# Gated networks of a two-block transformer step: the high weights multiply the high and the low input in one 512-column product

## What is computed

```
def _swiglu(xn, w_gate, w_up, w_down):
    return (jax.nn.silu(xn @ w_gate) * (xn @ w_up)) @ w_down
```

## Time and profile before

| | |
|---|---|
| median of 3 runs | 1210.81 us (1208.66 to 1210.96) |
| span of the profiled execution | 1209.8 us |
| TensorE busy | 1182.0 us, 98% of the span |
| VectorE (DVE), ScalarE (ACT) busy | 744.9 us (62%), 596.8 us (49%) |
| mean granted TensorE clock | 0.995 of full speed |
| `ffn1`: first product after the transposes to the first of `down1` | 608.84 to 718.35 us |
| `ffn2`: first product after the transposes | 1005.28 us |

### The profile page before, as it was taken

The page is one execution under the profiler, slowest core; times in us unless marked ns, Lnnn a source line. Parts: engine busy times, 40 slices in busy tenths (PEclk is TensorE's granted clock), DMA queues, the critical chain, the costliest instruction groups (busy, mean ns, idle before and its releaser), DMA issues.

```text
span 1209.8 us, 20515 instructions
## 1 busy us (share of the span) xinstructions
PE 1182.0 (98%) x8276; PEld 1101.8 (91%) x8276; DVE 744.9 (62%) x893; ACT 596.8 (49%) x804; POOL 118.1 (10%) x165
## 2 busy tenths in 40 slices
PE   7999999999998999999999999999999999999997
PEld 7998899999877999988999998789999989999875
DVE  5867556565856697864555454565766476554455
ACT  5675453445545576553454443454464355443342
POOL 5310201001025000000000000100400010000011
PEclk9999999999999999999999999999999999999999
DMA  8644343446545576555375555465465548655541
GB/s 234 208 142 137 105 140 122 123 140 222 182 136 174 155 221 195 178 199 183 122 244 178 189 189 177 152 207 179 140 213 196 166 140 263 195 177 174 196 139 64
DMA packets 156019, 208.57 MB, mean 172 GB/s; under 512 B 8608, under 2 KB 127405, under 8 KB 155949
## 3 DMA queue, kind: packets, MB, share of 16 engines
q1 hardware_dynamic: 152781, 198.92, 51.9%
q10 hardware_dynamic: 3072, 8.65, 2.1%
q0 software_dynamic: 96, 0.01, 0.1%
HBM read 206.50 MB, written 1.05 MB: 172 GB/s over the span
## 4 chain that ended last, share of the span: by engine, by line
PE 91%; DVE 4%; ACT 2%; POOL 1%; issue 1%; DMA 1%; POOLq 0%; DVEq 0%; SPq 0%; ACTq 0%
PE ACCP L776 26%; PE ACCP L778 26%; PE ACCP L777 26%; PE SMP L927 3%; PE SMP L920 2%; PE SMP L776 2%; PE SMP L778 2%; PE SMP L777 2%; DVE LO L1893 1%; ACT HI L1395 1%; POOL STAT L652 1%; DMA PRE_GAIN<-in_norm_mix_dram 1%; POOL STAT L651 0%; DVE XS L1929 0%; DVE X L2362 0%
## 5 line engine op out<-in xcount | busy, mean ns | idle before, releaser
L1893 DVE TENSOR_TENSOR LO<-RAW,HI 128x1024 fp32r<-128x1024 f32 x361 | 432.8, 1238 | 244.1 <-ACT HI L1395 242.8
L1395 ACT ACTIVATE HI<-RAW 128x1024 fp32r<-128x1024 f32 x366 | 368.4, 1053 | 225.5 <-PE ACCP L778 206.5
L776 PE MATMUL ACCP<-XH,HI 128*128 128x256 f32 x1536 | 437.4, 285 | 2.0 <-DVE XL L1938 2.0
L778 PE MATMUL ACCP<-XH,LO 128*128 128x256 f32 x1536 | 435.3, 283 | 0.0
L777 PE MATMUL ACCP<-XL,HI 128*128 128x256 f32 x1536 | 435.3, 283 | 0.0
L776 PEld LDWEIGHTS ACCP<-XH,HI 128*128 128x128 f32 x1536 | 295.4, 192 | 2.3 <-DVE LO L1893 2.2
L777 PEld LDWEIGHTS ACCP<-XL,HI 128*128 128x128 f32 x1536 | 295.5, 192 | 0.0
L778 PEld LDWEIGHTS ACCP<-XH,LO 128*128 128x128 f32 x1536 | 295.4, 192 | 0.0
L776 PE MATMUL ACCP<-HI,HH 128*128 128x512 f32 x264 | 105.0, 398 | 0.0
L778 PE MATMUL ACCP<-HI,HL 128*128 128x512 f32 x264 | 104.7, 396 | 0.0
L777 PE MATMUL ACCP<-LO,HH 128*128 128x512 f32 x264 | 104.6, 396 | 0.0
(11 more groups left out here) (388 smaller groups left out, 1560.3 us busy)
## 6 DMA issues: line engine op xcount, KB each, us to landing
RAW<-in_w_in_dram SPq DMA_DIRECT2D x104, 512.0 KB, 4.5
RAW<-in_w_up_dram SPq DMA_DIRECT2D x44, 512.0 KB, 4.5
RAW<-in_ffn_w_gate_dram SPq DMA_DIRECT2D x44, 512.0 KB, 4.7
RAW<-in_ffn_w_up_dram SPq DMA_DIRECT2D x44, 512.0 KB, 4.6
RAW<-in_ffn_w_down_dram SPq DMA_DIRECT2D x44, 512.0 KB, 4.2
RAW<-in_w_down_dram SPq DMA_DIRECT2D x22, 512.0 KB, 3.9
RAW<-in_w_out_dram SPq DMA_DIRECT2D x8, 512.0 KB, 4.5
RAW<-in_w_mkv_dram SPq DMA_DIRECT2D x8, 512.0 KB, 5.1
```

The lines of the kernel that those rows point to most:

```text
L776: pe.matmul(dst, lhs[0], rhs[0], start=start, stop=False)
L778: return pe.matmul(dst, lhs[1], rhs[0], start=False, stop=stop)
L1395: act.activation(HI[:, n % RING, half_of(half)], RAW[:, n % RAWS, half, :], ACT.Copy).then_inc(hi_ready, 1)
L1893: dve.tensor_tensor(LO[:, s, c], RAW[:, n % RAWS, half, :], HI[:, s, c].bitcast(f32), ALU.subtract).then_inc(lo_ready[s], 1)
```

## The change

For the blocks of `ffn1` and `ffn2` behind the opening (19 and 18 of them), the high and the low input become one tensor `XHL`, and the high weights multiply both in one product with 512 columns; the low weights multiply the high input as before. So each half of a block takes a whole PSUM bank, with the part of the low input in its second 256 columns, and a block takes two banks: an even block banks 0 and 1, an odd one banks 2 and 3. ACT copies the second parts of both banks to a new buffer `CROSS`, DVE adds them to the first parts (two additions of 128x256, which free the banks), and Silu and the gating product then work in SBUF. The opening's transposes also put each block's halves into two banks, and Silu and product of those blocks become two instructions of 128x256 each. Block one's `up` phase and all others stay as they are.

```diff
+CROSSED = ("ffn1", "ffn2")
+        elif phase in CROSSED:
+            for j in range(count):
+                acc(phase, j, j, 2 * (j % 2), 2 * (j % 2) + 1)
...
-        XH = sb("XH", [P, KT, SEQ], f32r)
-        XL = sb("XL", [P, KT, SEQ], f32r)
+        XHL = sb("XHL", [P, 2, KT, SEQ], f32r)
+        XH, XL = XHL[:, 0], XHL[:, 1]
...
+            def f_crossed(phase, t):
+
+                s = lo_is_ready(pe, phase, t)
+                acc_banks_free(pe, phase, t)
+                for half in range(2):
+                    bank = acc(phase, t, half)
+                    whole = bank.rearrange("p (n s) -> p n s", s=SEQ)
+                    for k in range(KT):
+                        c = slice(k * 256 + half * P, k * 256 + half * P + P)
+                        if k < KT - 1:
+                            pe.matmul(whole, HI[:, s, c], XHL[:, :, k, :], start=k == 0, stop=False)
+                            pe.matmul(bank[:, 0:SEQ], LO[:, s, c], XH[:, k, :], start=False, stop=False)
+                        else:
+                            pe.matmul(bank[:, 0:SEQ], LO[:, s, c], XH[:, k, :], start=False, stop=False)
+                            last = pe.matmul(whole, HI[:, s, c], XHL[:, :, k, :], start=False, stop=True)
+                last.then_inc(block_done, 1)
...
                     for half in range(2):
                         for t in range(NT):
-                            dst = acc(phase, Turn(j))[:, half * SEQ + t * P:half * SEQ + (t + 1) * P]
+                            if phase in CROSSED:
+                                dst = acc(phase, Turn(j), half)[:, t * P:(t + 1) * P]
+                            else:
+                                dst = acc(phase, Turn(j))[:, half * SEQ + t * P:half * SEQ + (t + 1) * P]
...
             def glu_steps(phase):
+                def cross(t, k):
+
+                    acc_is_done(act, phase, t.part(k, 2))
+                    act.activation(CROSS[:, k], acc_pair(phase, t.part(k, 2), 1), ACT.Copy).then_inc(cross_ready, 1)
+
                 def step(t):
-                    a, b = t.part(0, 2), t.part(1, 2)
-                    acc_is_done(act, phase, a)
-                    act.activation(UA[:, t.j % 2], acc(phase, a).rearrange("p (n s) -> p n s", s=SEQ),
-                                   ACT.Silu).then_inc(acc_bank(phase, a), 1)
-                    split_behind(phase, a)
+                    a, b, u = t.part(0, 2), t.part(1, 2), t.j % 2
+                    if is_open(phase, a):
+                        acc_is_done(act, phase, a)
+                        for i in range(2):
+                            act.activation(UA[:, u, i, :], acc(phase, a, i)[:, 0:SEQ], ACT.Silu).then_inc(acc_bank(phase, a, i), 1)
+                        split_behind(phase, a)
+                    else:
+                        cross(t, 0)
+                        split_behind(phase, a)
+                        acc_is_taken(act, phase, a, 1)
+                        act.activation(UA[:, u], UA[:, u], ACT.Silu).then_inc(a_gated, 1)
+                    if not is_open(phase, b):
+                        cross(t, 1)
                     split_behind(phase, b)
-                    acc_is_taken(act, phase, b)
+                    act.wait_ge(h_ready, hidden_pairs(phase, t))
                     ffn_hi(t)
...
             def glu_steps(phase, pairs):
+                def whole(t, k, dst):
+
+                    part = t.part(k, 2)
+                    dve.wait_ge(cross_ready, crossings(phase, t, k))
+                    for i in range(2):
+                        dve.tensor_tensor(dst[:, i, :], acc(phase, part, i)[:, 0:SEQ], CROSS[:, k, i, :],
+                                          ALU.add).then_inc(acc_bank(phase, part, i), 1)
+
                 def step(t):
-                    a, b = t.part(0, 2), t.part(1, 2)
+                    a, b, u = t.part(0, 2), t.part(1, 2), t.j % 2
+                    if not is_open(phase, a):
+                        whole(t, 0, UA[:, u])
                     split_behind(phase, a)
-                    acc_is_done(dve, phase, b)
-                    acc_is_taken(dve, phase, a)
-                    dve.tensor_tensor(UB[:, t.j % 2], acc(phase, b).rearrange("p (n s) -> p n s", s=SEQ), UA[:, t.j % 2],
-                                      ALU.mult).then_inc(acc_bank(phase, b), 1)
+                    if is_open(phase, b):
+                        acc_is_done(dve, phase, b)
+                        for i in range(2):
+                            acc_is_taken(dve, phase, a, i)
+                            ins = dve.tensor_tensor(UB[:, u, i, :], acc(phase, b, i)[:, 0:SEQ], UA[:, u, i, :], ALU.mult)
+                            ins.then_inc(acc_bank(phase, b, i), 1)
+                        acc_is_taken(dve, phase, b, 1)
+                        dve.sem_inc(h_ready, 1)
+                    else:
+                        whole(t, 1, UB[:, u])
+                        if is_open(phase, a):
+                            acc_is_taken(dve, phase, a, 1)
+                        else:
+                            dve.wait_ge(a_gated, gatings(phase, t))
+                        acc_is_taken(dve, phase, b, 1)
+                        dve.tensor_tensor(UB[:, u], UB[:, u], UA[:, u], ALU.mult).then_inc(h_ready, 1)
                     split_behind(phase, b)
```

More of the change, by code:

```diff
@@ L304, in build @@
         UB = at("UB", 48, [P, 2, 2, SEQ])
+        CROSS = at("CROSS", 68, [P, 2, 2, SEQ])
         OPENED = at("OPENED", 56, [P, NT, 4 * 256])
@@ L375, in build @@
         post_sq, tap_done, dve_mix = sems("post_sq tap_done dve_mix")
+        cross_ready, a_gated = sems("cross_ready a_gated")
         ln_mean, ln_sq, ln_ready = sems("ln_mean ln_sq ln_ready")
@@ L448, in acc_is_done, with is_open, crossings, gatings @@
             eng.wait_ge(block_done, t.count(lambda j: ACC_LAST[phase, j] + 1))
+        def is_open(phase, t):
+            return t.i is None and t.j < F_OPEN[phase]
+        def crossings(phase, t, k):
+            before = sum(COUNT[p] - F_OPEN[p] for p in CROSSED[:CROSSED.index(phase)])
+            return t.count(lambda j: before + 2 * j + k + 1 - F_OPEN[phase])
+        def gatings(phase, t):
+            opened_a = [-(-F_OPEN[p] // 2) for p in CROSSED]
+            n = CROSSED.index(phase)
+            before = sum(FT // 2 - opened_a[i] for i in range(n))
+            return t.count(lambda j: before + j + 1 - opened_a[n])
+        def hidden_pairs(phase, t):
+            return t.count(lambda j: PAIRS.index(phase) * (FT // 2) + j + 1)
+        def acc_pair(phase, t, part):
+            b = ACC_BANKS[phase, t.j][0]
+            return ACCP[:, b:b + 2, part * SEQ:(part + 1) * SEQ]
         def tile_is_done(eng, phase, m):
@@ L1253, in ffn, with one @@
             def ffn(r, up, down, behind, before):
+                def one(t):
+                    if up in CROSSED:
+                        f_crossed(up, t)
+                    else:
+                        f_gemm(up, t, XH, XL)
                 def step(t):
                     for k in range(2):
-                        f_gemm(up, t.part(k, 2), XH, XL)
+                        one(t.part(k, 2))
                 def hidden_ready(k):
@@ L1262, in ffn @@
                 for j in range(F_OPEN[up], 4):
-                    f_gemm(up, Turn(j), XH, XL)
+                    one(Turn(j))
                 repeat(pe, 2, FT // 2, 2, step)
```

## The result

The changed kernel takes 1215.4 us (median), the kernel before 1211.2 us in the same series: a ratio of 1.0034, 95% interval 1.0023 to 1.0045. It is 4 us slower, where 2 us faster was forecast, and it lies above the forecast's range.

A forecast was written before the change was run, and what follows sets the result against it. The prediction took TensorE to bound the kernel. Wide products at -8.0 us, ACT and DVE at nothing and openings at +6.0 gave -2.0, from a 1210.8 us median to 1208.8 us, range 1207.0 to 1213.3.

The forecast's parts named there:

- What bounds the kernel: Whole kernel: 91% of the span lies on TensorE, so the distance between products and any added TensorE idle time count.
- Part 1, the wide product: Steady blocks of `ffn1` and `ffn2`: one 512-column product replaces two of 256, saving 13.5 ns in each of 592 steps, 8.0 us.
- 226.7 + 120.1: Steady blocks: one wide plus one narrow product makes a step of 346.8 ns, where three narrow ones took 360.3.
- home of the stationary side: Wide products: weights in tensors of their own (`HI`, `LO`) should cost 226.7 ns, those in the arena 234.1.
- The rule that the Trainium skill gives: Isolated products at full clock: columns over 2.4 plus about 2.5 ns; by it 592 steps would save only 1.5 us.
- Part 2, ACT and DVE in the steady blocks at nothing: Steady blocks: added copies and additions cost nothing, with cover of 3.7 us on the banks and 2.6 us on loads.
- Part 3, the openings: Starts of `ffn1` and `ffn2`: waits for banks to be freed by gating cost 2.5 + 3.5 = 6.0 us.
- The rival with the clock: Openings of `ffn1` and `ffn2`: TensorE's clock falls, 1.7 us lost; one fall gives 1210.5 us, two 1212.2; chance 0.20.
- The sum: Whole kernel: -8.0 + 6.0 = -2.0 us, so a forecast of 1208.8 us.
- The 234 ns rival: Steady blocks: the wide product costs 234.1 ns, so -3.6 + 6.0 = +2.4 us, 1213.2 us; chance 0.11.

## Why the prediction was wrong, point by point

- **What bounds the kernel** was right: TensorE, before and after.
- **Part 1, the wide product, was mis-sized.** The term was -8.0 us and measured -4.6 (7.8 ns a step, not 13.5). The price of 226.7 ns for weights from `HI` was right for a stream of its own kind. The step that failed is the sum "226.7 + 120.1": it added two prices, each taken from a stream of one width, for a stream in which the widths take turns. There the pair costs 352.5 ns, because the first wide products behind a narrow one are dearer. The rows chosen for the price hid it, since they begin 1.8 us behind the change of width; the first products of that phase show 233 ns. The argument "home of the stationary side" chose the right row, but home stood for the offset from 128 bytes.
- **The rule that the Trainium skill gives** ("TensorE: Matmul & The Clock Gate", section "Back-to-back issue gap", 2.5 ns on top of the columns) did not hold here either: in a stream of wide products each carries 13.4 ns on top of its columns, as the earlier trace rows had it.
- **Part 2, ACT and DVE in the steady blocks at nothing,** was right, with 0.60 us for the copy and 0.75 for the additions.
- **Part 3, the openings,** was right in the profile: 2.5 and 3.4 us against 2.5 and 3.5 forecast, with the waits on the engines named. For `ffn1` some of that is luck. Of eight profiles of kernels with this opening three have 3.70 us from the first transpose to block 3, and five have 4.4 to 5.2, since Silu of block 0 stands behind a load that may land late. The prediction read that load's landing in one profile and took it as fixed.
- **The rival with the clock** came true, in both openings, with 1.6 us each against 1.7 forecast. This is the second step that failed: the sum has no term for the clock, since the rival stood at 0.20, against which the prediction said that transposes break the idle stretches. Short groups of transposes, 8 and then 4 in 3.7 us, did not keep the clock up.
- **The sum.** With -4.6, +5.9 and the clock's +3.2 the forecast's own working gives +4.5 us, and the measured ratio is +4.1. The 234 ns rival alone gave 1213.2 and the clock rival alone 1212.2 for two falls; the range ended at 1213.3 because it took no two of them together. Both came: the clock in full, and the dearer wide product in size (4.6 us saved, nearer to that rival's 3.6 than to 8.0), though not for that rival's reason.

## What to carry to other kernels

A product's price from a stream of one width is a lower bound, not a price, for a stream that mixes widths; read it at the change of width too, and group the products of one width if the accumulation allows it. When a ring gets shallower, look first at where it is filled all at once (an opening), ask for each wait there what else stands ahead of it on the releasing engine, loads included, and count with the price of a clock fall behind every stretch that leaves TensorE half idle. Let a tensor that serves as the stationary side of 512-column products start at a multiple of 128 bytes; here its 6.4 us outweighed the 1.6 us that 64 beyond one gives on the moving side. When a ratio is off by a few us, compare the two profiles phase by phase, the phases that no edit touches included.

## What the runs showed of the hardware that was not expected

- The start address of the stationary side costs time with 512-column fp32r products: 226.7 ns at a multiple of 128 bytes, 233.3 at 64 beyond one, 234.3 at 96 beyond one. As the moving side the same input at 96 beyond one cost nothing: 120.0 ns a product of 256 columns (418 of them in 50.2 us in the kernel with the input behind the arena), as before.
- The start address of the moving side matters too, the other way: with 256 columns a product cost 120.0 ns with `HH` at a multiple of 128 bytes or at 96 beyond one, and 117.8 at 64 beyond one (432 products in `mix_out`).
- Wide and narrow products in turn cost 352.5 ns a pair, 5.7 more than in streams of their own (226.7 + 120.1). Behind a return to 512 columns the first five products cost 233, 236, 228, 232 and 231 ns, the later ones 226.7.
- Twelve transposes in 3.7 us, and sixteen in 5.2 us, with no idle stretch over 1.9 us, were each followed by 1.2 GHz for most of the next 4 us. In the kernel with DVE's other order twelve in 3.8 us, with an idle stretch of 2.1 us, were not.
